# One room for the gathered tokens, a ninth place for expert weights, and a third segment block for the SSD term between chunks

## What is computed

```
acs = cumsum(a)                                   # per chunk of 128 tokens, per head (32 heads)
y_diag = einsum(cb, exp(acs_l - acs_s) for s <= l, xs)         # within a chunk
states = einsum(bm, exp(acs_end - acs_s), xs)                  # what a chunk leaves behind
y_off  = einsum(cm, previous chunk's states, exp(acs_l))       # what the next chunk reads of it
y = y_diag + y_off

for e in range(64):                                # experts; each token uses 8 of them
    gu = t @ w_exp_gu[e]                           # 1024 x 512
    h = silu(gu[:, :256]) * gu[:, 256:]
    y = y + gates[:, e:e + 1] * (h @ w_exp_down[e])   # 256 x 1024
```

## Time and profile before

| What | Value |
|---|---|
| Median of 3 runs | 978.56 us (977.16 to 978.86) |
| The profiled execution, its own time | 978.27 us |
| Its span, first to last instruction | 976.4 us |
| PE busy | 962.7 us, 99% |
| DVE busy | 520.6 us, 53% |
| ACT busy | 392.4 us, 40% |
| POOL busy | 33.6 us, 3% |
| Transfers | 292.42 MB, mean 299 GB/s; 420 to 428 GB/s in the last 17 of the 40 slices but the last |
| First gate-and-up matmul of the expert part | 509.7 us |

### The profile page before, as it was taken

How to read it: one execution, slowest core, us unless ns; L and a number is a source line. 1 busy time by engine, 2 the same in 40 slices (tenths; PEclk the granted TensorE clock), 3 DMA queues, 4 the chain that set the end, 5 groups by cost and what they waited for, 6 DMA issues and landing times.

```text
span 976.4 us, 15340 instructions
## 1 busy us (share of the span) xinstructions
PE 962.7 (99%) x6318; PEld 694.3 (71%) x6319; DVE 520.6 (53%) x1073; ACT 392.4 (40%) x707; POOL 33.6 (3%) x46
## 2 busy tenths in 40 slices
PE   9999999999999999999999999999999999999995
PEld 8999999999999999999984444444444444444342
DVE  6988556868689966865675433223222322332124
ACT  6776435656678644455341122112211221221113
POOL 0000101221100000000000000000000000000000
PEclk9999999999999999999999999999999999999998
DMA  8585434433354545656969999999999999999993
GB/s 319 189 303 182 176 143 154 133 132 133 140 199 163 183 173 190 243 216 254 395 256 355 423 424 425 426 423 428 422 429 423 426 425 424 424 428 419 419 420 142
DMA packets 35061, 292.42 MB, mean 299 GB/s; under 512 B 3880, under 2 KB 6064, under 8 KB 7472
## 3 DMA queue, kind: packets, MB, share of 16 engines
q1 hardware_dynamic: 34208, 286.19, 73.6%
q0 software_dynamic: 784, 5.24, 1.4%
HBM read 290.36 MB, written 2.63 MB: 300 GB/s over the span
## 4 chain that ended last, share of the span: by engine, by line
PE 96%; DVE 2%; DMA 1%; issue 0%; ACT 0%; DVEq 0%; ACTq 0%
PE stream L1683 33%; PE stream L2041 23%; PE stream L2065 12%; PE stream L1708 9%; PE work L2030 6%; PE stream L2051 1%; PE stream L1982 1%; PE stream L1984 1%; PE work L1809 1%; PE work L1797 1%; PE work L2018 1%; PE stream L2058 1%; PE stream L1988 1%; PE work L1915 1%; PE work L1897 1%; PE stream L1990 1%
## 5 line engine op out<-in xcount | busy, mean ns | idle before, releaser
L1068 DVE TENSOR_TENSOR w_lo<-raw,w_hi 128x1024 fp32r<-128x1024 f32 x142 | 171.4, 1225 | 52.3 <-ACT w_hi L737 51.8
L2041 PE MATMUL stream<-ring,xg 128*64 128x512 f32 x640 | 197.1, 592 | 0.0
L737 ACT ACTIVATE w_hi<-raw 128x1024 fp32r<-128x1024 f32 x142 | 147.2, 1052 | 57.5 <-DMA raw<-in_wdense 40.4
L1683 PE MATMUL stream<-xT_hi,w_hi 128*128 128x256 f32 x560 | 159.4, 285 | 0.0
L1683 PE MATMUL stream<-xT_lo,w_hi 128*128 128x256 f32 x560 | 157.9, 282 | 0.0
L1683 PE MATMUL stream<-xT_hi,w_lo 128*128 128x256 f32 x560 | 157.7, 282 | 0.0
L2041 PEld LDWEIGHTS stream<-ring,xg 128*64 128x64 f32 x640 | 62.5, 137 | 90.9 <-issue 90.7
L1683 PEld LDWEIGHTS stream<-xT_hi,w_hi 128*128 128x128 f32 x560 | 106.2, 190 | 3.9 <-issue 3.1
L1683 PEld LDWEIGHTS stream<-xT_hi,w_lo 128*128 128x128 f32 x560 | 105.9, 189 | 0.0
L1683 PEld LDWEIGHTS stream<-xT_lo,w_hi 128*128 128x128 f32 x560 | 105.6, 189 | 0.0
L1554 DVE TENSOR_TENSOR hh<-h,stream 128x256 f32<-128x256 f32 x32 | 13.5, 422 | 170.3 <-ACT h L997 170.3
(11 more groups left out here) (396 smaller groups left out, 1997.2 us busy)
## 6 DMA issues: line engine op xcount, KB each, us to landing
ring<-in_wstream SPq DMA_DIRECT2D x46, 2048.0 KB, 18.8
raw<-in_wdense SPq DMA_DIRECT2D x72, 1024.0 KB, 4.8
ring<-in_wstream SPq DMA_DIRECT2D x28, 1024.0 KB, 19.9
place_e<-in_wstream SPq DMA_DIRECT2D x9, 2048.0 KB, 17.5
place_m<-in_wstream SPq DMA_DIRECT2D x12, 1024.0 KB, 16.7
place_c<-in_wstream SPq DMA_DIRECT2D x12, 1024.0 KB, 18.6
place_w<-in_wstream SPq DMA_DIRECT2D x12, 1024.0 KB, 17.1
place_x<-in_wstream SPq DMA_DIRECT2D x12, 1024.0 KB, 19.0
```

What stands on the lines that cost most here:

```text
L737: nc.scalar.activation(w_hi[:, q % ROUNDED, :], raw[:, q % 6, :], ACT.Copy).then_inc(w_rounded, 1)
L1068: tt(w_lo[:, q % 6, :], raw[:, q % 6, :], w_hi[:, q % ROUNDED, :].bitcast(F32), ALU.subtract).then_inc(w_rest, 1)
L1683: last = mm(S[n % 4][:, 0:SEQ], w[:, b, :], a[:, kb, :], start=(kb + j == 0), stop=(kb == chunks * KB - 1 and j == len(parts) - 1))
L2041: last = mm(S[2][e * SLOTS:(e + 1) * SLOTS, :], feature_block(buf, kb)[:, col + e * SLOTS:col + (e + 1) * SLOTS], tiles[e][kb // 4][:, kb ...
```

## The change

It has three parts.

1. **The term between chunks.** A third run of sums is made (`sums_across`: the second chunk's running sums plus the first chunk's total) and used for a third segment block in the loop: three `head_sums` on POOL, three segment matmuls on PE, three minima and three multiplications on DVE, three exponentials on ACT in each pass. The product with xs of chunk 0 is accumulated into chunk 1's output by 4 more matmuls. What falls away: `decay_end` and its matmul, `xend`, `mask_wide`, `head_mask`, `fac`, `yo` and the 4 matmuls that made them meet. The lists are put in another order: segment block 0, then the logits, then blocks 1 and 2; DVE's minima of blocks 1 and 2 come after the logits' maxima; the attention's transposes come after the third output block; the values go to W[3] and not W[1].
2. **One room.** `xg` is one room of 16 KiB. A pair frees 8 cells, and the two gathers in that pair are written there; group 0 lies by feature block, the later groups in turn by other strides. The copy's target is seen as [128, 4, 128].
3. **A ninth place** (`place_r`, `place_g`) lies where the second room was, for tile x % 9 == 8. Its first tile, 8, is issued in two halves: one after the one-hots of the second group, at the head of the refills, and one after `residual_done`. It always comes in halves. Tiles of one piece now are 11 to 80. Tiles from 89 on are shifted to places 0 to 6, and the shared expert's weights (`wsd`) go to where the ninth place's first half was.

The core of the diff:

```diff
-RING = 8
+RING = 9
+SHIFT = 3 * PAIRS - 7
...
+        def place_of(x):
+            return x % RING if x < SHIFT else x - SHIFT
...
-        by_need = 25
+        by_need = 24
...
             expert_halves(7, 7)
+            sp.wait_ge(onehot_done, 2 * TB)
+            expert_half(8, 8, 0)
...
+                if pair == 0:
+                    sp.wait_ge(residual_done, 4)
+                    expert_half(8, 8, 1)
+                if x + 2 == SHIFT:
+                    return
                 sp.wait_ge(down_mm, pair * 2 + 2)
...
+            def segment(i, t):
+                pe.wait_ge(gdec_done, SEGS * i + t + 1)
+                if t == 2:
+                    pe.wait_ge(decay_step, 2 * SEGS * i + 1)
+                elif i and t == 1:
+                    pe.wait_ge(av_cp, i)
+                elif i == 0:
+                    pe.wait_ge(xs_cp, 8)
+                else:
+                    pe.wait_ge(y_done, i)
+                mm(W[2 + t % 2][:], minus_sums[:, t % 2, :], head_sums[:, t]..., start=True, stop=True).then_inc(seg_mm, 1)
...
+                segment(i, 0)
                 if i >= 1:
                     pe.wait_ge(attnT_cp, i)
-                    pe.wait_ge(av_cp, i)
...
+                segment(i, 1)
+                segment(i, 2)
...
-                    for t in range(TB):
+                    for t, s, n in ((0, 0, 0), (1, 1, 1), (1, 0, 2)):
...
-                              mask_wide[:, 2 * j:2 * j + 2, :].rearrange("p h e -> p (h e)"),
-                              minus_sums[:, 1, :], start=True, stop=True)
-                last.then_inc(off_mm, 1)
+                feature_major(kind, k0 + 2, xT_r)
                 pe.wait_ge(attn_done, i + 1)
...
-                mm(W[1][:, 0:P], attnT[:, 0:P], v[:, 0, head], start=True, stop=True)
+                mm(W[3][:, 0:P], attnT[:, 0:P], v[:, 0, head], start=True, stop=True)
```

201 lines of the change are left out of this document (86 added, 115 removed).

## The result

The changed kernel takes 980.18 us (median of 20 runs, 979.18 to 981.28) against 978.36 (20 runs of before beside them): a ratio of 1.0018, 95% interval 1.0012 to 1.0024. It is 1.8 us slower, where 977.8 was forecast with 979.9 as the upper end. By the prediction's bound of 0.2% that is still "the same", but it is clear of the noise, the sign was wrong and the time lies outside the range. The profiled execution took 980.20 us with a span of 978.3, against 978.27 and 976.4.

The account below looks back on a forecast made before the run. PE was taken to bound the kernel, the expert weight stream nearly as tight; -1.7 (PE's work) + 0.9 (ninth place) = -0.8 us against the profiled 978.27 gave 977.5, or 977.8 as median; range 976.0 to 979.9.

Parts of the forecast that it names:

- PE's sum: PE's own work over the loop and ahead of it: +0.7 - 2.2 - 0.2 = -1.7 us, between -2.5 and -0.5.
- the ninth place's sum: End of the weight stream in the expert part: -1.7 + 1.9 + 0.7 = +0.9 us, between 0 and +2.6.
- the middle of a pass: Head loop, last projection matmul to next block: term between chunks replaced by four matmuls; -0.27 us a pass, -2.2 in eight.
- the better fill: Weight stream from 516 to 540: a fuller queue should raise 396 GB/s to 427; -1.7 us, at worst 0.
- What bounds the kernel: Whole kernel: PE bounds it throughout; the expert weight stream is as long as PE's work, so lateness costs in full.
- The boundary of two passes: Head loop: o_tok wait goes, one segment matmul is added; +0.07 us in seven passes, +0.23 in the first, +0.7 total.
- The cover of 0.6 us: Head loop: third multiplication ends 6.9 us after segment block 0, PE needs it at 7.5; costed at nothing.
- The rival of the vector chain: Head loop: PE waits 0.5 us for the third multiplication in each of 8 passes; +4, so 981.8; chance 0.06.
- Ahead of the loop: Before the head loop: the matmul for decay_end goes, -0.2 us.
- The later first issue: SP's list, head of refills: first refill waits for the second group's one-hots, later issues queue behind it; +1.9 us.
- Nine tiles more in halves: Expert weight stream: 46 one-piece tiles instead of 55, each tile in halves 0.08 us longer; +0.7 us.
- The stream paces the end: Rival: queue stays thin from 516 to 540, +2.6 us at the end; 980.7 with PE's lower-bound gain; chance 0.13.

Follow-up runs that it names:

- loop_only: Kernel before with only the change's loop part (third segment block, new pass order, no decay_end), two rooms, eight places: 977.89 us against 978.17 (0.9999).
- one_room: Changed kernel without the ninth place, with eight places and the old refill order; new loop and one room stay: 977.76 us (0.9997).
- combined: Changed kernel with the SP order of eighth_split, each block's xs products awaiting only their own multiplication, one-piece tiles up to 86: 977.49 us against 978.39 (0.9991).
- eighth_split: Changed kernel, pair 0's four refill halves issued first, the ninth place's first-tile halves either side of the one-piece tile: 978.13 us against 978.39 (0.9996).
- eighth_later: Changed kernel with both halves of the ninth place's first tile issued behind pair 0's four refill halves, after residual_done: 979.59 us (1.0014).
- one_load_on: Changed kernel with 64 one-column matmuls (256 instructions, 16 KB of code) added on PE ahead of the first pass's logits: 1006.9 us.

## Why the prediction was wrong, point by point

**The steps that failed.** For the profiled execution 977.5 was forecast and 980.20 measured, 2.7 us more. PE's sum has 1.5 of them (its lead was to be 1.7 and was 0.19), the ninth place's sum 1.25 (+0.9 was to be the lateness at the end and +2.15 was). In PE's sum the mis-sized term is the middle of a pass, -2.2 in the forecast and -0.9 measured. In the ninth place's it is the better fill, -1.7 in the forecast and -1.2 measured, and a price of 0.96 us that the sum did not have. Their working follows.

**What bounds the kernel: right.** The stream was as long as PE's work, and what it lost came out at the last pairs.

**The boundary of two passes: right.** 0.07 more was worked out. From segment block 0 to the second projection matmul it is 188.48 - 186.52 = 1.96 us, before 1.89 (186.56 to 188.45). In the first pass it was +0.23, as said. The logits start 0.41 behind block 0 and not 0.33; the rest came in less behind them.

**The middle of a pass: mis-sized.** -0.27 was forecast and -0.11 measured. The 24 records take 194.24 to 195.70, 0.44 more than the 16 of before (0.43 forecast), and the transposes' own change of kinds about 0.09 (0.1). Two terms failed. The 0.07 us for a change from the products to the term that was gone did not come back. And the step to the products took 0.09 us more, a wait.

**The cover of 0.6 us: gone, and this is where the wait came from.** PE was ready 7.63 us behind block 0 (7.5 forecast; its 1.65 for the first output block is no more than the 1.66 of before, so it left out the boundary's own +0.07), and the multiplication ended at 7.66 and not 6.9. The failed term is "the logits' maxima now begin at 1.3 and end 1.8 us later": they began at 1.39 and took 2.56 us, because of POOL's third block on the step on `a_neg`. The sentence that POOL's third block "lies in idle time" was true of POOL and said nothing on DVE. The rival of the vector chain named the place; the chain ended 0.03 us behind the point at which PE was ready and the products started 0.06 behind that, 0.09 us in seven passes: 0.6 us in all and not 4.

**PE's sum: failed, by the middle of a pass.** Ahead of the loop -0.18 (-0.2 forecast). The loop, its first boundary in it, gave 0.35 us and not 1.5. Of PE's whole -1.7 a lead of 0.19 us was left at the first gate-and-up matmul, since this execution also began 0.14 later (its first weights) and lost 0.2 between the loop and the experts. Such pieces differ between executions: loop_only and one_room came to it at 508.87 and 508.63.

**The ninth place: failed, by the better fill and what it costs.** The later first issue was right, 1.9 us behind the first gate-and-up. Nine tiles more in halves cost 0.7 in the forecast; by the mean of the engines 0.5 us are lost between the ninth half and the end, and in combined five tiles given back are worth 445.00 - 444.64 = 0.36, or 0.07 each, as assumed. "Better fill ... -1.7 us" failed twice. Only 1.2 us of it came: the queue was full, but against a full queue the kernel before had lost 1.45 and not 1.7 (eighth_split), and the first transfer took 0.2 us longer than there from its issue to the engines' mean (4.83 against 4.60). And the full queue has a price that the sum had not: an engine that is held up by a code load catches up where the queue runs dry behind pair 0's halves (one_room, eighth_later), and in the changed kernel it does not (1.60 us behind the mean from the third half to the ninth). The slowest engine is 1 us further behind the others at the end. That the same engine is hit again by every eighth load is argued from the distances of the loads. -1.7 + 1.9 + 0.7 = +0.9 became +2.15.

**The rivals.** "The stream paces the end" gave 980.7 with little of PE's gain and 980.2 is what was measured. Its size was right by luck: PE's gain was small, as it said, but the queue did not stay thin (426 GB/s from 518 on), and other losses at the end took the place of the missing fill. It had 0.13 of the chances.

**What would show it.** The first refill at 515.13, pairs 0 to 27 unchanged at 14.13 us, and no wait on `o_tok`: as said. The last two pairs' gate-and-up were to take 7.3 to 7.6 and not 6.9 us; the last alone took 8.3 (6.87 + 1.45), and the three ahead of it 0.2 to 0.3 more.

## What to carry to other kernels

Where a stream of transfers was as long as the work on it, its end moved with its first issue (1.9 us at the head, 2.2 at the end); a wait for a new buffer belongs behind the issues that need no new buffer, and eighth_split got the whole loss back by that alone. A deeper ring gave this saturated stream nothing, and keeping its queue full took away the gap in which a late transfer engine had caught up. An engine's "idle time" hides added work only if that work takes nothing from its neighbours: of a step added on POOL, look at what DVE does in the same microsecond.

## What the runs showed of the hardware that I had not expected

- Code is loaded while the kernel runs, in packets of 16 KB on queue 8 (51 of them in the whole program), about 1.0 us of one transfer engine each. In a full queue the last of the 16 updates stayed 1.6 us behind their mean for as long as it was full; where it ran dry in eighth_later it went from 1.60 to 0.22. Landings were late by up to 1.4 us. The largest delays came behind loads that are eight apart, in the five kernels of the table and in eighth_later.
- A step of DVE on 4 elements per partition took 0.93 us beside a POOL multiplication and 0.17 with POOL idle, in one and the same kernel. It stands in the profile as a busy time of DVE, not as a wait.
- Matmuls of one column cost 0.2 us a record, and the granted clock fell while PE ran them, from 1.00 in the microsecond ahead. In one_load_on 127 of their records lie between 155.17 and 180.52; the granted clock of that stretch and of the ones behind it (windows, columns as above):

```profile
156.00:180.00 24.00, 24.00 (x120) 24.00 (x120) 0.05 (x1) 1.84 (x3) 0.37 (x1) 0.53 0.12 44
180.00:190.00 10.00, 10.00 (x70) 9.02 (x72) 6.92 (x16) 4.42 (x14) 2.04 (x2) 0.77 0.00 0
190.00:192.00 2.00, 2.00 (x30) 1.83 (x27) 1.89 (x8) 1.03 (x2) 0.00 (x0) 1.00 0.54 164
```

  PE was busy throughout, and yet it ran at 0.53, all but the lower of its two levels (1.2 GHz); it was back at the full 2.4 GHz by 190.
